# Backward chunk states of a Mamba-2 scan: the two-buffer loop written out, with four chunk buffers and three state buffers

## What is computed

```python
decay_to_end = jnp.exp(a_cum[:, :, -1:] - a_cum)
chunk_states = jnp.einsum('bclgn,bclgrp->bcgrpn', bc, X * decay_to_end[..., None])
chunk_decay = jnp.exp(a_cum[:, :, -1])

def step(h, inp):
    st, dec = inp
    return h * dec[..., None, None] + st, h
...
h_final, h_enter = lax.scan(step, h_init, (jnp.moveaxis(chunk_states, 1, 0), jnp.moveaxis(chunk_decay, 1, 0)))
```

## Time and profile before

| | |
|---|---|
| Median of three runs | 2640.83 us |
| Time of the profiled execution | 2632.1 us |
| Its span from first to last instruction | 2630.5 us |
| Mean granted TensorE clock | 0.941 |
| TensorE busy | 2303.4 us, 88% |
| VectorE busy | 1386.4 us, 53% |
| ScalarE busy | 1019.2 us, 39% |
| First DMA of `back_states` issued | 553.47 us |
| Last store of `back_states` issued | 601.80 us |
| First DMA of `mixer` issued | 606.08 us |

### The profile page before, as it was taken

How to read it: one execution, slowest core, us unless ns; L and a number is a source line. 1 busy time by engine, 2 the same in 40 slices (tenths; PEclk the granted TensorE clock), 3 DMA queues, 4 the chain that set the end, 5 groups by cost and what they waited for, 6 DMA issues and landing times. The chain is left out here.

```text
span 2630.5 us, 41317 instructions
## 1 busy us (share of the span) xinstructions
PE 2303.4 (88%) x15978; PEld 2105.5 (80%) x15978; DVE 1386.4 (53%) x2211; ACT 1019.2 (39%) x1816; POOL 237.0 (9%) x319
## 2 busy tenths in 40 slices
PE   4899999955998998834999999999999999999960
PEld 2878888844777777633999999999999999999960
DVE  3655534154555556564555556555565555655523
ACT  3632222214445434302444444444444344443423
POOL 0000000010100100001011101011110111101001
PEclk8999999987999999965999999999999999999985
DMA  8533442244223223104456566566565665655627
GB/s 268 184 112 131 138 133 85 106 141 146 97 90 130 88 88 125 67 17 146 160 169 188 184 186 184 163 184 185 184 190 165 179 188 184 197 166 176 181 66 255
DMA packets 318408, 396.32 MB, mean 151 GB/s; under 512 B 11742, under 2 KB 272878, under 8 KB 316286
## 3 DMA queue, kind: packets, MB, share of 16 engines
q1 hardware_dynamic: 289326, 291.93, 34.9%
q0 software_dynamic: 24848, 94.98, 12.0%
q10 hardware_dynamic: 4160, 8.39, 0.9%
HBM read 318.12 MB, written 77.14 MB: 150 GB/s over the span
## 5 line engine op out<-in xcount | busy, mean ns | idle before, releaser
L2127 DVE TENSOR_TENSOR experts_wlo<-experts_raw,experts_whi 128x2048 fp32r<-128x2048 f32 x192 | 440.2, 2293 | 423.2 <-ACT experts_whi L2071 423.2
L2009 PE MATMUL experts_ps_r<-experts_xhi,experts_whi 128*128 128x272 f32 x2048 | 605.4, 296 | 5.4 <-DVE experts_xlo L2181 5.4
L2009 PE MATMUL experts_ps_r<-experts_xhi,experts_wlo 128*128 128x272 f32 x2048 | 593.9, 290 | 0.0
L2009 PE MATMUL experts_ps_r<-experts_xlo,experts_whi 128*128 128x272 f32 x2048 | 590.2, 288 | 0.0
L2009 PEld LDWEIGHTS experts_ps_r<-experts_xhi,experts_whi 128*128 128x128 f32 x2048 | 386.2, 189 | 8.4 <-DVE experts_xlo L2181 5.5
L2009 PEld LDWEIGHTS experts_ps_r<-experts_xlo,experts_whi 128*128 128x128 f32 x2048 | 387.2, 189 | 0.0
L2009 PEld LDWEIGHTS experts_ps_r<-experts_xhi,experts_wlo 128*128 128x128 f32 x2048 | 386.1, 189 | 0.0
L2071 ACT ACTIVATE experts_whi<-experts_raw 128x2048 fp32r<-128x2048 f32 x192 | 366.2, 1907 | 16.4 <-DMA experts_raw<-in_w_gate 14.5
L2009 PE MATMUL experts_ps_r<-experts_hhi,experts_whi 128*128 128x272 f32 x1024 | 299.7, 293 | 0.2 <-DVE experts_hlo L2201 0.2
L2009 PE MATMUL experts_ps_r<-experts_hhi,experts_wlo 128*128 128x272 f32 x1024 | 296.2, 289 | 0.0
L2009 PE MATMUL experts_ps_r<-experts_hlo,experts_whi 128*128 128x272 f32 x1024 | 294.7, 288 | 0.0
(11 more groups left out here) (381 smaller groups left out, 3576.1 us busy)
## 6 DMA issues: line engine op xcount, KB each, us to landing
experts_raw<-in_w_gate SPq DMA_DIRECT2D x64, 1024.0 KB, 5.0
experts_raw<-in_w_up SPq DMA_DIRECT2D x64, 1024.0 KB, 5.0
experts_raw<-in_w_down SPq DMA_DIRECT2D x64, 1024.0 KB, 5.3
mixer_mt<-mixed SPq DMA_DIRECT2D x17, 1024.0 KB, 7.2
shared_whalf<-in_w_ada SPq DMA_DIRECT2D x16, 1024.0 KB, 5.3
mixed<-front_acc POOLq DMA_DIRECT2D x9, 1024.0 KB, 4.2
resid<-early_xin POOLq DMA_DIRECT2D x17, 512.0 KB, 3.8
mixer_xs<-resid SPq DMA_DIRECT2D x17, 512.0 KB, 8.1
```

Source lines behind the costliest of these rows:

```text
L2009: mm = pe.matmul(dst, w[:, c % RING, kk, cols], r[:, kk, :], start=(kk == 0 and q == 0), stop=(kk == KD - 1 and q == 2))
L2127: dve.tensor_tensor(wlo[:, c % RING, :, :], raw[:, c % RAW, :, :], whi[:, c % RING, :, :].bitcast(F32), ALU.subtract).then_inc(wlo_done, 1)
```

## The change

The loop of every engine in `back_states` is written out as a Python loop with constants: no hardware loop, no registers, no `settled`, and the chain semaphore of VectorE is waited for against constants. `xb` gets four buffers, so the load of step n waits for step n-4 to be turned and the first four loads go out at once. `hb` gets three buffers, so the addition of step n waits for the store of state n-2. The PSUM buffers, `xw`, `bt` and `tmp` stay as they are, as do all shapes, and the order of the operations on TensorE and VectorE. The `mixer` code isn't touched.

```diff
--- before.py
+++ after.py
@@ -1046,59 +1046,47 @@
 
 def back_states(nc, g, io):
 
-
-
-
     N = NT - 2
+    NB_X, NB_H = 4, 3
     with ExitStack() as ctx:
         k = Kit(nc, ctx, "back_states")
         st = k.sb("st", [P, 2, 4, NS])
-        xb = k.sb("xb", [P, 2, 6, P])
+        xb = k.sb("xb", [P, NB_X, 6, P])
         xw = k.sb("xw", [P, 2, 512])
         bt = k.sb("bt", [P, 2, 256])
         tmp = k.sb("tmp", [P, 512])
-        hb = k.sb("hb", [P, 2, 512])
+        hb = k.sb("hb", [P, NB_H, 512])
         ps_x = k.ps("ps_x", [P, 2, 512])
         ps_b = k.ps("ps_b", [P, 2, 512])
         ps_s = k.ps("ps_s", [P, 2, 512])
-        settled = k.sem("settled2")
         st_loaded, st_turned, st_copied = k.sem("st_loaded"), k.sem("st_turned"), k.sem("st_copied")
-        xb_loaded = k.sems("xb_loaded", 2)
+        xb_loaded = k.sems("xb_loaded", NB_X)
         turned, xw_done, bt_done = k.sem("xb_turned"), k.sem("xw_done"), k.sem("bt_done")
         s_done, h_chain, h_done = k.sem("bs_done"), k.sem("bh_chain"), k.sem("bh_done")
-        hb_stored = k.dma_sems("hb_stored", 2)
+        hb_stored = k.dma_sems("hb_stored", NB_H)
         mixed = io["mixed"]
         block = ctx.enter_context(nc.Block())
 
         @block.gpsimd
         def _(pool):
-            pool.wait_ge(settled, 1)
-
-            def store(n, b, j):
-                if first_tiles(n, 1):
+            for n in range(N + 1):
+                if n == 0:
                     pool.wait_ge(st_copied, 2)
                 else:
-                    hold(pool, settled, (h_done, n))
-                pool.dma_start(io["back"][bass.ds(n, 1), :, :].rearrange("o p c -> (o p) c"), hb[:, b, :]
-                               ).then_inc(hb_stored[b], 16)
-
-            over_tiles(pool, N + 1, [(store, 0)])
-            for b in range(2):
-                pool.wait_ge(hb_stored[b], 16 * (N + 1) // 2)
+                    pool.wait_ge(h_done, n)
+                pool.dma_start(io["back"][n, :, :], hb[:, n % NB_H, :]).then_inc(hb_stored[n % NB_H], 16)
+            for b in range(NB_H):
+                pool.wait_ge(hb_stored[b], 16 * len(range(b, N + 1, NB_H)))
 
         @block.sync
         def _(sp):
-            sp.nop().then_inc(settled, 1)
             for d, name in enumerate(("state_ssm_fwd", "state_ssm_bwd")):
                 sp.dma_start(st[:, d, :, :], io[name][0, 0].rearrange("(a h) d n -> (h d) a n", a=4)).then_inc(st_loaded, 16)
-
-            def load(n, b, j):
-                if not first_tiles(n, 2):
-                    hold(sp, settled, (turned, n - 1))
-                sp.dma_start(xb[:, b, :, :], mixed[8:14, :, bass.ds(n * -P + 16 * P, P)].rearrange("s p t -> p s t")
-                             ).then_inc(xb_loaded[b], 16)
-
-            over_tiles(sp, N, [(load, 0)])
+            for n in range(N):
+                if n >= NB_X:
+                    sp.wait_ge(turned, n - NB_X + 1)
+                sp.dma_start(xb[:, n % NB_X, :, :], mixed[8:14, :, P * (16 - n):P * (17 - n)].rearrange("s p t -> p s t")
+                             ).then_inc(xb_loaded[n % NB_X], 16)
 
         @block.tensor
         def _(pe):
@@ -1108,21 +1096,22 @@
                     ins = pe.transpose(ps_s[:, d, P * a:P * a + P], st[:, d, a, :], g.ident[:, :])
             ins.then_inc(st_turned, 1)
 
-            def turn(n, b, j):
-                pe.wait_ge(xb_loaded[b], 16 * j + 16)
-                if not first_tiles(n, 2):
+            def turn(n):
+                pe.wait_ge(xb_loaded[n % NB_X], 16 * (n // NB_X) + 16)
+                if n >= 2:
                     pe.wait_ge(xw_done, n - 1)
                     pe.wait_ge(bt_done, n - 1)
                 for a in range(4):
-                    pe.transpose(ps_x[:, b, P * a:P * a + P], xb[:, b, a, :], g.ident[:, :])
+                    pe.transpose(ps_x[:, n % 2, P * a:P * a + P], xb[:, n % NB_X, a, :], g.ident[:, :])
                 for a in range(2):
-                    ins = pe.transpose(ps_b[:, b, P * a:P * a + P], xb[:, b, 4 + a, :], g.ident[:, :])
+                    ins = pe.transpose(ps_b[:, n % 2, P * a:P * a + P], xb[:, n % NB_X, 4 + a, :], g.ident[:, :])
                 ins.then_inc(turned, 1)
 
-            def states(n, b, j):
+            def states(n):
+                b = n % 2
                 pe.wait_ge(xw_done, n + 1)
                 pe.wait_ge(bt_done, n + 1)
-                if first_tiles(n, 2):
+                if n < 2:
                     pe.wait_ge(st_copied, 2)
                 else:
                     pe.wait_ge(h_done, n - 1)
@@ -1131,48 +1120,51 @@
                                    xw[:, b, 256 * a:256 * a + 256], start=True, stop=True)
                 mm.then_inc(s_done, 1)
 
-            over_tiles(pe, N, [(turn, 0), (states, 1)])
+            for n in range(N + 1):
+                if n < N:
+                    turn(n)
+                if n:
+                    states(n - 1)
 
         @block.scalar
         def _(act):
             act.wait_ge(st_turned, 1)
             act.activation(g.hf[:, 1, :], ps_s[:, 0, :], ACT.Copy).then_inc(st_copied, 1)
             act.activation(hb[:, 0, :], ps_s[:, 1, :], ACT.Copy).then_inc(st_copied, 1)
-
-            def copy_b(n, b, j):
+            for n in range(N):
                 act.wait_ge(turned, n + 1)
-                if not first_tiles(n, 2):
+                if n >= 2:
                     act.wait_ge(s_done, n - 1)
-                act.activation(bt[:, b, :], ps_b[:, b, 0:256], ACT.Copy).then_inc(bt_done, 1)
-
-            over_tiles(act, N, [(copy_b, 0)])
+                act.activation(bt[:, n % 2, :], ps_b[:, n % 2, 0:256], ACT.Copy).then_inc(bt_done, 1)
 
         @block.vector
         def _(dve):
-            chain = Chain(dve, h_chain)
-
-            def weigh(n, b, j):
+            def weigh(n):
                 dve.wait_ge(turned, n + 1)
-                if not first_tiles(n, 2):
+                if n >= 2:
                     dve.wait_ge(s_done, n - 1)
-                w = g.tab[:, bass.ds(n * -1 + 16, 1), T_WEND + H:T_WEND + HH].rearrange("p o h -> p (o h)")
-                dve.tensor_tensor(heads(xw[:, b, :]), heads(ps_x[:, b, :]), per_head(w), ALU.mult).then_inc(xw_done, 1)
-
-            def carry(n, b, j):
-                chain.start(n)
-                if first_tiles(n, 1):
+                w = g.tab[:, 16 - n, T_WEND + H:T_WEND + HH]
+                dve.tensor_tensor(heads(xw[:, n % 2, :]), heads(ps_x[:, n % 2, :]), per_head(w), ALU.mult).then_inc(xw_done, 1)
+
+            def carry(n):
+                frm, to = n % NB_H, (n + 1) % NB_H
+                if n == 0:
                     dve.wait_ge(st_copied, 2)
                 else:
                     dve.wait_ge(h_done, n)
-                dec = g.tab[:, bass.ds(n * -1 + 16, 1), T_DEC + H:T_DEC + HH].rearrange("p o h -> p (o h)")
-                chain.link(dve.tensor_tensor(heads(tmp[:, :]), heads(hb[:, b, :]), per_head(dec), ALU.mult))
+                dec = g.tab[:, 16 - n, T_DEC + H:T_DEC + HH]
+                dve.tensor_tensor(heads(tmp[:, :]), heads(hb[:, frm, :]), per_head(dec), ALU.mult).then_inc(h_chain, 1)
+                dve.wait_ge(h_chain, n + 1)
                 dve.wait_ge(s_done, n + 1)
-                if not first_tiles(n, 1):
-                    dve.wait_ge(hb_stored[1 - b], (j + b) * 16)
-                dve.tensor_tensor(hb[:, 1 - b, :], tmp[:, :], ps_s[:, b, :], ALU.add).then_inc(h_done, 1)
-                chain.end(n)
-
-            over_tiles(dve, N, [(weigh, 0), (carry, 1)])
+                if n + 1 >= NB_H:
+                    dve.wait_ge(hb_stored[to], 16 * ((n + 1) // NB_H))
+                dve.tensor_tensor(hb[:, to, :], tmp[:, :], ps_s[:, n % 2, :], ALU.add).then_inc(h_done, 1)
+
+            for n in range(N + 1):
+                if n < N:
+                    weigh(n)
+                if n:
+                    carry(n - 1)
 
 
 def mixer(nc, g, io):
```

## The result

The changed kernel takes 2627.3 us, median of 5 runs (2625.85 to 2629.05), against 2640.83 us for the kernel before (5 runs, 2639.68 to 2641.42). The direction and the mechanism were right; the size was not, and the question of the experiments is where the other 4.5 us come from.

A forecast was written before the change was run, and what follows sets the result against it. Two chunk buffers' load waits were taken to bound back_states; 9.0 us from pace and start, 0.4 from POOL's store, 0.2 from the last addition made 9.6, less 0.6: 2640.8 - 9.0 = 2631.8 us, range 2629.0 to 2637.0.

The forecast's parts named there:

- What bounds the stage: In back_states, waits for chunk loads set the pace before; afterwards VectorE would, at 1.93 us a chunk.
- the landing formula for stores: Pace where hb stores hold it: (1.17 us + landing) / number of buffers; with three, landings up to 4.62 us cost nothing.
- the pace before: Weighing of chunk 2 at 565.88 to chunk 14 at 597.43 us in one profile: 12 steps of 2.63 us.
- The start: Weighing of chunk 2 in back_states would move from 565.88 to 564.7 us.
- The tail: End of back_states: 0.4 us from POOL's last store and 0.24 us from the last addition's wait for a store.
- The 0.6 us I took off: Deduction from the 9.6 us gain because TensorE's 2.82 us wait at 591.30 might be peculiar to the profile.
- The range: Kernel time after the change between 2629.0 and 2637.0 us.
- Rival A: DMA engines set back_states' pace at 261 GB/s, chunk 14 weighed at 593.0, kernel 2636.0 us; chance 0.15.
- Rival B: Four loads crowd chunk 0 (2.8 us late) and lengthen store landings to 8.1 us, kernel 2647.6 us; chance 0.05.
- the slack of 6.7 us: Time a chunk load may take to land with four buffers before TensorE waits, against a longest landing of 5.7 us.
- Rival C: TensorE stays at 1.2 GHz in back_states, 3.01 us a chunk, kernel 2643.8 us; chance 0.03.
- Rival D: Gain smaller than forecast: median is of other executions or an unseen wait takes half, 2637 to 2640 us; chance 0.05.

The follow-up runs named there:

- e3: Changed kernel with two state buffers instead of three (loop written out, four chunk buffers): 2635.19 us, ratio interval 0.9974 to 0.9994 to the kernel before.
- e2: Changed kernel with two chunk and two state buffers, so only the loop written out: 2640.53 us, ratio interval 0.9986 to 1.001 to the kernel before.
- e1: The kernel before, unchanged, run again: 2639.26 us, median of 11 runs, ratio interval 0.9984 to 1.0004 to itself.
- e5: The changed kernel again, no edit: 2627.71 us, median of 10 runs, ratio interval 0.9939 to 0.9972 to the kernel before.
- e12: The kernel before, unchanged, a fourth profile only: 2639.91 us in one run.
- e10: The kernel before, unchanged, a third profile only: 2643.86 us in one run.
- e9: Changed kernel with half of the weighing moved from VectorE to ScalarE: 2628.83 us, median of 11 runs, ratio interval 0.9945 to 0.9969 to the kernel before.
- e11: The changed kernel, no edit, a third profile only: 2627.86 us in one run.

## Why the prediction was wrong in its size

**What bounds the stage: right.** The waits moved as stated, from chunk loads to VectorE; 1.92 us a step; the clock held at 1.00 in every stretch of 5 us from 565 to 590; the landing formula for stores held in e3 within 0.1 us a step.

**The step that failed is the pace before**, "12 steps of 2.63 us", 31.6 us. Four profiles have 31.6, 33.0, 34.7 and 32.8, a mean of 33.0 us. After, I said 588.4 - 564.7 = 23.7 us; the three profiles have 24.9, 23.2 and 23.1, a mean of 23.7. The side of the change that had to be worked out was met; the side that could be read was taken from one execution that was quick by 1.4 us in this term. Part of the 33.0 may be the hardware loop itself, which the forecast put at nothing: e2, written out with the old buffers, took 31.4. That stays open.

**The start** was put at 1.2 us of gain (565.88 to 564.7). The means are 12.7 and 10.7 us from the first DMA to chunk 2, a gain of 2.1. I let TensorE begin turning chunk 2 only when its products had ended, and took 563.77 from the profile of the forecast, where these products took 1.86 us; in the other three of before they took 1.13 to 1.17, in the three after 1.46, 1.03 and 1.13. In all three profiles after, VectorE went from the addition to this weighing without idle time. Products of chunk 0, in the profile of the forecast and in e5:

```profile
561.91 1.86 PE L1130 MATMUL back_states_ps_s<-back_states_xw,back_states_bt 128*128 128x256 f32 x4
```

```profile
561.74 1.03 PE L1119 MATMUL back_states_ps_s<-back_states_xw,back_states_bt 128*128 128x256 f32 x4
```

**The tail** was put at 0.6 us. The means are 9.0 and 8.0 us, a gain of 1.0. The 0.4 us of POOL's store are there (0.29 us behind the addition, not 0.71); the rest is one wait of the last addition for a store, which was 0.24 us in the profile of the forecast, 1.7 in e1, 0.4 in e12 and nothing in e10.

Sum: 9.3 + 2.1 + 1.0 = 12.4 us, where 7.85 + 1.2 + 0.6, rounded to 9.6, were forecast. The 1.1 us from there to the 13.5 that were measured lie well inside the interval of the result (9 to 17 us) and need no cause.

**The 0.6 us I took off went the wrong way.** I argued that one long wait of the profile was peculiar to it, and so that the median would gain less. But that execution lay 8.7 us under the median of the runs, and this was the thing to explain: its stage was 2.1 us shorter than the mean of the four, and its transposes in `selection` were on the quick side, 4.7 us from the slow one (below). Where an execution is quicker than the median, it is more likely that its waits are short than long, and a change that removes waits then gains more than its profile shows. Here the forecast should have been 9.6 plus about 2.

**The range** was too narrow. Its fast end, 2629.0, was a best case worked out from the quick profile, with nothing for the spread of the executions: the three runs shown lay within 1.5 us of each other, but 32 runs of the same kernel spread over 14 us, and the interval of the measured gain is 7.7 us wide. The bound of 0.2% for what can be told from no change was about right: 10 or 11 runs gave half-widths of 0.1 to 0.17%.

**Rival A** (the DMA engines hold the pace at 261 GB/s) is refuted: 358 to 372 GB/s in stretches of the three profiles of the changed kernel. The Trainium skill, "DMA: Bandwidth & Descriptors", Specifications, gives a limit of HBM per core of about 358 GB/s; the trace agrees to within 4%, a little above it. The rival was right in one thing, that this limit stands close behind VectorE's (e9).

**Rival B** (crowding): landings grew a little. The medians of the four profiles before are 4.2 to 4.7 us for loads and 2.8 to 3.8 for stores, of the three after 4.7 to 5.7 and 3.8 to 4.2; that is under the slack of 6.7 us and the bound of 4.62. The longest, 7.0 and 6.0 in the first profile after, are over them; VectorE waited 1.8 us for stores in that execution, and 0.2 us and not at all in the other two. The same page of the Trainium skill, Queues, rings and completion order, has an engine take turns between queues; the stores' landing of 4.2 us behind four queued loads agrees with it, without proving it. **Rival C** didn't occur: granted 1.00 from 565 to 590 us. **Rival D** neither, though half of its ground was there: the median was of other executions, and they gained more than the profiled one, not less.

## What to carry to other kernels

Count for each buffer the whole loop from its release to its next use, landing included, and compare it with the pace of the busiest engine: the loop with the largest quotient sets the time, and mending one of two nearly equal loops gave a fifth to a third of what both gave in the stage (1.9 and 2.8 us of 9.5, from e2 to the mean of the three after). Landings must be taken with a margin: from a share of the DMA engines of 0.9 to one of 1.1 their medians grew by about a fifth on average, and the longest store from 4.6 to 6.0 us. And before making a forecast from a single profile, set its own time beside the median: if they differ by about as much as the gain in question (here 8.7 us against 9.0), the waits read from it may be those of an unusual execution, and a second profile of the kernel before is worth its cost.

## What the runs showed of the hardware

The same program on the same chip spreads over 13 to 18 us in groups of 10 to 32 runs, and one place makes up to 4.7 us of it. In `selection` TensorE does 32 transposes after a stretch of sparse work. Their rows in the profile of the forecast, in e10 (the same kernel), in after and in e3:

```profile
1139.19 3.84 PE L1728 MATMUL selection_ps_row<-kept_ident,kept_mod 128*128 128x128 f32 x32
```

```profile
1145.72 6.62 PE L1728 MATMUL selection_ps_row<-kept_ident,kept_mod 128*128 128x128 f32 x32
```

```profile
1133.16 3.84 PE L1720 MATMUL selection_ps_row<-kept_ident,kept_mod 128*128 128x128 f32 x32
```

```profile
1136.43 6.72 PE L1720 MATMUL selection_ps_row<-kept_ident,kept_mod 128*128 128x128 f32 x32
```

They take 3.84 us at a granted clock of 1.00 (1133 to 1137 us in after), or 6.4 to 6.7 at a mean grant of 0.55 (1145.7 to 1152.3 us in e10), and 5.32 in e5, between the two:

```profile
1132.01 5.32 PE L1720 MATMUL selection_ps_row<-kept_ident,kept_mod 128*128 128x128 f32 x32
```

The stretch from the mixer's last chunk load to the experts' first load is 125.2 to 125.4 us with the first and 129.8 to 130.1 with the second. What TensorE is given to do before is the same in all of them, but the row just ahead of the transposes, 17 small ones, has parted already: 1.19 or 1.20 us in the seven profiles with 3.84, and 1.96 or 1.97 in the other seven. In after and in e3:

```profile
1132.04 1.20 PE L1716 MATMUL selection_ps_log<-kept_ident,kept_logits 16*128 16x16 f32 x17 [0.61 <-PEq L1172]
```

```profile
1134.53 1.97 PE L1716 MATMUL selection_ps_log<-kept_ident,kept_logits 16*128 16x16 f32 x17 [0.61 <-PEq L1172]
```

Of the 14 profiles seven have 3.84 us, five 6.4 to 6.7, and two lie between. The kernel before had both sides, two profiles each. The changed kernel had 3.84, 5.32 and 3.84 and not once the slow side; of the seven profiles with a stage of 49 us or more five are slow, of the seven with a shorter one none. Whether the shorter stage moves the later clock, which would add a microsecond or two to what the change is worth, or whether this is chance, 14 profiles don't say, and what decides it wasn't tried.

Two more numbers. With loads in rows of 512 bytes and stores in rows of 2 KB together, the 16 DMA engines carried up to 372 GB/s over 5 us (e11). And the time from a store's issue to its landing, 256 KB, was 2.2 us with nothing beside it, at the end of the stage in every run, and up to 6.0 in the middle of it.
